# Where a three-mixer trunk runs its weight-stream k-tiles, and which engine applies the rotary sine

## What is computed

```python
for l in range(DEPTH):                       # DEPTH = 2
    mod = (silu(c) @ w_ada[l] + b_ada[l])    # six vectors of 1024 per sequence
    h = rmsnorm(x, norm_mix[l]) * (1 + sc_m) + sh_m
    proj = h @ w_in[l]
    o_a = gated_delta(silu(conv4(q_a, k_a, v_a)), g, beta)     # A
    q_b = _rope(q_b, pos); k_b = _rope(k_b, pos) * HEAD_K ** -0.5
    o_b = retention(q_b, k_b, v_b)                             # B
    o_c = hgrn2(q_c, f_gate, v_c)                              # C
    o_i = norm(o_i) * gate_i                                   # each, per head
    merged = sum(sigmoid(merge_i) * (o_i @ w_branch[l, i]))
    x = x + gt_m * (merged @ w_out[l])
    h = rmsnorm(x, norm_ffn[l]) * (1 + sc_f) + sh_f
    x = x + gt_f * ((silu(h @ wg) * (h @ wu)) @ w_down[l])
# _rope: concatenate([x1 * cos - x2 * sin, x1 * sin + x2 * cos])
```

## Time and profile before

| | us |
|---|---|
| three executions | 2683.02, 2673.51, 2682.92 |
| their median | 2682.92 |
| the profiled execution | 2676.24 |
| its span, first to last instruction | 2674.2 |
| PE busy | 2516.4 (94%) |
| POOL busy | 1546.2 (58%) |
| DVE busy | 1015.0 (38%) |
| ACT busy | 456.3 (17%) |
| mean granted TensorE clock | 0.967 of full |

### The profile page before, as it was taken

The page is one execution under the profiler, slowest core; times in us unless marked ns, Lnnn a source line. Parts: engine busy times, 40 slices in busy tenths (PEclk is TensorE's granted clock), DMA queues, the critical chain, the costliest instruction groups (busy, mean ns, idle before and its releaser), DMA issues. The chain is left out here.

```text
span 2674.2 us, 47818 instructions
## 1 busy us (share of the span) xinstructions
PE 2516.4 (94%) x20318; PEld 2404.7 (90%) x20318; DVE 1015.0 (38%) x1479; ACT 456.3 (17%) x856; POOL 1546.2 (58%) x1292
## 2 busy tenths in 40 slices
PE   6989999999999899999989899999999998999997
PEld 4879888989989899999978799799899798999997
DVE  3663424150743442222255633421427435222223
ACT  3421222121121120000034222310211212000001
POOL 2542235557547757777755322355664486777775
PEclk8999999999999999999989899999999898999999
DMA  8720014223324512322365210142241142223222
GB/s 350 243 80 28 29 41 126 65 64 106 93 58 132 208 64 91 85 90 89 87 225 184 64 34 28 47 123 76 64 138 50 55 152 64 89 87 90 87 87 77
DMA packets 167043, 263.92 MB, mean 99 GB/s; under 512 B 14128, under 2 KB 83376, under 8 KB 165040
## 3 DMA queue, kind: packets, MB, share of 16 engines
q1 hardware_dynamic: 166832, 260.88, 30.9%
HBM read 239.65 MB, written 21.17 MB: 98 GB/s over the span
## 5 line engine op out<-in xcount | busy, mean ns | idle before, releaser
L796 PE MATMUL gemm_psum<-h_hi_lo,w_hi_lo 128*128 128x272 f32 x12000 | 1626.3, 294 | 42.5 <-DVE h_hi_lo L1326 31.6
L796 PEld LDWEIGHTS gemm_psum<-h_hi_lo,w_hi_lo 128*128 128x128 f32 x12000 | 1557.9, 193 | 89.6 <-issue 78.7
L525 POOL TENSOR_TENSOR w_hi_lo<-w_raw,consts 128x512 fp32r<-128x512 f32 (+1 forms) x644 | 691.7, 1074 | 1052.2 <-PE gemm_psum L796 966.9
L527 POOL TENSOR_TENSOR w_hi_lo<-w_raw,w_hi_lo 128x512 fp32r<-128x512 f32 (+1 forms) x644 | 855.8, 1329 | 50.4
L1970 ACT ACTIVATE tiles<-gemm_psum 128x544 f32<-128x544 f32 (+1 forms) x188 | 116.3, 623 | 1184.7 <-PE gemm_psum L796 1184.1
L796 PE MATMUL gemm_psum<-ffn_hi_lo,w_hi_lo 128*128 128x272 f32 x2112 | 264.8, 287 | 0.0
L796 PEld LDWEIGHTS gemm_psum<-ffn_hi_lo,w_hi_lo 128*128 128x128 f32 x2112 | 264.4, 188 | 0.0
L1952 DVE TENSOR_TENSOR tiles<-gemm_psum,tiles 128x544 f32<-128x544 f32 x44 | 31.9, 725 | 386.7 <-PE gemm_psum L796 376.2
L796 PE MATMUL gemm_psum<-o_hi_lo,w_hi_lo 128*128 128x272 f32 x1152 | 154.0, 290 | 0.0
L796 PEld LDWEIGHTS gemm_psum<-o_hi_lo,w_hi_lo 128*128 128x128 f32 x1152 | 147.1, 189 | 0.0
L1970 ACT ACTIVATE scratch<-mix_psum 128x512 f32<-128x512 f32 (+3 forms) x112 | 58.9, 547 | 359.7 <-PE mix_psum L1073 174.8
(11 more groups left out here) (234 smaller groups left out, 1915.0 us busy)
## 6 DMA issues: line engine op xcount, KB each, us to landing
w_raw<-in_w_gu SPq DMA_DIRECT2D x176, 256.0 KB, 2.7
tiles<-in_w_ada SPq DMA_DIRECT2D x64, 512.0 KB, 4.9
w_raw<-in_w_merge SPq DMA_DIRECT2D x96, 256.0 KB, 2.6
w_raw<-in_w_first SPq DMA_DIRECT2D x68, 256.0 KB, 5.2
w_raw<-in_w_ret SPq DMA_DIRECT2D x64, 256.0 KB, 2.7
w_raw<-in_w_hg SPq DMA_DIRECT2D x64, 256.0 KB, 2.7
w_raw<-in_w_dn SPq DMA_DIRECT2D x64, 256.0 KB, 2.6
w_raw<-in_w_merge SPq DMA_DIRECT2D x96, 128.0 KB, 2.1
```

Source lines behind the costliest of these rows:

```text
L525: pool.tensor_tensor(hi, src, ones[:, 0:1].broadcast_to([P, words]), ALU.mult).then_inc(hi_done, 1)
L527: pool.tensor_tensor(lo, src, hi.bitcast(F32), ALU.subtract).then_inc(split_done, 1)
L796: mm = pe.matmul(GP[:, 2 * (tile % 2) + h, 0:HALF], whl[:, n % SLOTS, a, j * P:(j + 1) * P], rhs[:, b, step, h * HALF:(h + 1) * HALF], sta ...
```

## The change

Five things, the same in both layers except where said.

1. The fills of mixer A are bounded by `RG_END`, no more by `Z_END`, and more k-tiles stand in them: 4 for 2 ahead of the last join, 5 for 2 ahead of `branch_ready`, 4 for 2 ahead of the query products of each pair of chunks. The `drain(Z_END)` ahead of the sampled chunk is gone. The fills ahead of the sum of squares in the three norms are 2, 4, 6 for 2, and those behind it 7, 6, 5 for 3.
2. The sine product of a `rope` tile moves from DVE to POOL, behind the split of the fourth slab after that tile. DVE adds the two products one tile later, tile 7 with the first `gdn_z` tile.
3. The copy of the gate columns (L1520 before) moves ahead of the last convolution.
4. DVE waits for the stored prompt state inside `start_branch`, behind `branch_ready`.
5. POOL splits slabs 1 to 3 of layer 0 in the layer's block, not in the first block. SP loads the four ada groups with 16 k-tiles of stream between them, and the first one eight k-tiles earlier in its list.

```diff
+SUMS_FILL = (2, 4, 6)
+ROOT_FILL = (7, 6, 5)
...
         def _(pool):
             pool.wait_ge(sig("ones_landed"), 16)
-            for n in range(SLOTS):
-                split_slab(pool, n)
+            split_slab(pool, 0)
...
-                fill(4 * H + KD, BASE["silu0"])
+                fill(4 * H, BASE["silu0"])
                 if ahead:
                     sp.wait_ge(sig("h_ready"), 2 * KD)
                     for i in range(4):
                         sp.dma_start(ada_group[i], w_ada_first[l + 1, i]).then_inc(sig(f"ada_group_landed_{i}"), 16)
+                        fill(2 * KD, BASE["silu0"])
...
             def _(pool):
+                for n in range(1, SLOTS if l == 0 else 0):
+                    split_slab(pool, n)
                 for n in range(slab_base + SLOTS, slab_end):
                     split_slab(pool, n)
+                    for i in range(8):
+                        if n == slab_base + last_slab(BASE["rope"] + i) + SLOTS:
+                            tmp = swap_temp[i % 2]
+                            pool.wait_ge(sig("swapped"), i + 1)
+                            pool.tensor_tensor(tmp, tmp, C[:, C_SIN:C_DRET], ALU.mult).then_inc(sig("sine_applied"), 1)
...
-                    fill(2, limit)
+                    fill(SUMS_FILL[n], limit)
                     four_sums(sq_o[n], 0, True, True)
-                    fill(3, limit)
+                    fill(ROOT_FILL[n], limit)
...
                     i = TILES[tile][1]
                     wait_tile(tile)
                     k.next(sig("swapped"))
-                    out, tmp = brt[:, RQ + i, :], swap_temp[i % 2]
-                    dve.tensor_tensor(halves(out), gp(tile), halves(C[:, C_COS:C_SIN]), ALU.mult
-                                      ).then_inc(buf_free[tile % 2], 1)
-                    k.link(dve.tensor_tensor(tmp, tmp, C[:, C_SIN:C_DRET], ALU.mult))
+                    k.link(dve.tensor_tensor(halves(brt[:, RQ + i, :]), gp(tile), halves(C[:, C_COS:C_SIN]), ALU.mult))
+                    release_buffer(tile)
+                    if i:
+                        rope_sum(i - 1)
+
+                def rope_sum(i):
+                    out = brt[:, RQ + i, :]
+                    k.next(sig("sine_applied"))
                     k.settle()
-                    dve.tensor_tensor(out, out, tmp, ALU.add).then_inc(sig("rope_slot_free"), 1)
+                    dve.tensor_tensor(out, out, swap_temp[i % 2], ALU.add).then_inc(sig("rope_slot_free"), 1)
...
                     say("branch_ready")
+                    if stored:
+                        dve.wait_ge(sig("stored_prompt"), 16 * stored)
                     k.link(dve.memset(ST[:, :, :], 0.0))
...
                 def gdn():
-                    fill(2, Z_END)
+                    fill(5, RG_END)
```

More of the change, by code:

```diff
@@ L1010, in _ @@
                         per_head(3, lambda c: pe.transpose(B[:, 3, c * P:(c + 1) * P], ROW[:, cols(c)], ident))
-                fill(2, Z_END)
+                fill(4, RG_END)
                 ada_join(ADA_LOTS - 1)
@@ L1021, in _ @@
                         four_spreads(j, half)
-                        fill(2, Z_END)
+                        fill(2, RG_END)
                 def gdn_turn(c):
@@ L1365, in _, with release_buffer @@
                 sum_base = [0]
+                def release_buffer(tile):
+                    k.settle()
+                    dve.nop().then_inc(buf_free[tile % 2], 1)
                 def rope(tile):
@@ L1406, in evacuate @@
                         rope(tile)
+                    elif tile == BASE["gdn_z"]:
+                        rope_sum(7)
                     elif name == "hg_f":
@@ L1483, in gate_rows, with columns_of @@
                     say("gate_rows_ready")
+                def columns_of(bank, parts):
+                    return bank.rearrange("p (c j x) -> p c j x", j=4, x=32)[0:parts, :, 0:3, 0:4]
                 for n in range(1, NCQ + 1):
@@ L1507, in _ @@
                         rows_of()
+                        k.next(full[3])
+                        k.link(dve.tensor_copy(COL[:, 0:NCH, :].rearrange("p c (j x) -> p c j x", j=3), columns_of(B[:, 3, :], P)))
+                        release(3)
                 def bank_pair(i):
@@ L1513, in bank_pair @@
                     return B[:, b:b + 2, 0:HALF], b
-                def columns_of(bank, parts):
-                    return bank.rearrange("p (c j x) -> p c j x", j=4, x=32)[0:parts, :, 0:3, 0:4]
-                fill(2, Z_END)
-                k.next(full[3])
-                k.link(dve.tensor_copy(COL[:, 0:NCH, :].rearrange("p c (j x) -> p c j x", j=3), columns_of(B[:, 3, :], P)))
-                release(3)
+                fill(4, RG_END)
                 k.next(full[2])
@@ L1548, in _, with start_branch @@
                         release_four()
-                        fill(2, Z_END)
+                        fill(2, RG_END)
                 k.next(sig("gate_exps"))
                 k.link(dve.tensor_tensor(CE[:, :, 8:12], CE[:, :, 0:4], COL[:, :, 4:8], ALU.mult))
-                def start_branch(tiles):
+                def start_branch(tiles, stored=0):
                     k.settle()
@@ L2027, in evacuate @@
                     elif name == "ret_v":
+                        act.wait_ge(sig("rope_slot_free"), 10)
                         take(tile, brt[:, RV + i, :], ACT.Copy)
```

57 lines of the change are left out of this document (26 added, 31 removed).

## The result

The changed kernel takes 2651.69 us, the median of four executions (2650.57 to 2652.75), where the kernel before takes 2681.53 (2673.51 to 2683.02, four executions, one more than shown above). The medians are 30 us apart. The ratio given for them is 0.9906, with a 95% interval of 0.9878 to 0.9935, which is 25 us, as much as the span fell in the profiled executions. So the gain is 25 to 30 us, where the forecast had 46, and the forecast of 2636 was 15.7 too low. The range holds the time. The number is nearest to the rival in which the clock stays low (2656), but not by that rival's way: it wanted all 26.6 us of the waits and nothing of the clock. That the two add up to nearly its number is luck.

A forecast was written before the change was run, and what follows sets the result against it. PE was taken as the bound, with its waits and lower clock as the time to gain. Waits 24.8 + 6.4 - 4.6 + clock 19.6 = 46.2 us off the median of 2682.9 gave 2636.7, stated as 2636; range 2604 to 2664.

The forecast's parts named there:

- the rival in which the clock stays low: Whole run: the waits left bring the lower clock back, so only 26.6 us are gained, giving 2656; chance 0.15.
- entry of A: Ahead of mixer A's gate columns, per layer: two k-tiles fit into the 3.71 us wait; waits fall by 1.8.
- rope tiles 0 and 1: Fourth spread and `branch_ready` in mixer A, per layer: these tiles end earlier, ahead of awaited steps; waits rise by 2.1 us.
- products: First pair in mixer A, per layer: tile 1 no longer delays the query products, tile 2 delays the next step; 0.7 us gained.
- levels and second pair: Mixer A, per layer: fewer delays from rope tiles; 0.6 us gained in the levels and 1.2 in the second pair.
- norm of A: Norm of mixer A, per layer: four more k-tiles cover the 2.47 us wait for the rows; 2.5 gained.
- start of B: Start of mixer B, per layer: DVE's 2.42 us wait for the stored state moves behind `branch_ready` and is covered; 2.4 gained.
- norm of B: Norm of mixer B, per layer: k-tiles take in 3.8 us, but `hg_f` tiles delay the root and state products; 1.0 gained.
- norm of C: Norm of mixer C, per layer: four more k-tiles cover the 2.88 us wait, two the 1.54; 4.3 gained.
- `w_out`: Among the `out` tiles, once: with the ada groups spaced out, the 6.38 us wait goes; 6.4 gained.
- start (first k-tile): Start of layer 0, once: it starts 2.3 us earlier, but POOL's six operations among DVE's cost 6.9; net 4.6 lost.
- clock, both layers: Fourteen half-clock stretches of 1.4 us go, six per layer in the mixers, two behind the 6.38 wait; 19.6 gained.

The follow-up runs named there:

- e2: The changed kernel with 3 k-tiles ahead of the sums in the norm of B, not 4, and 7 behind them, not 6: 2639.5 us.
- e8: The changed kernel with 4, 3, 6 k-tiles ahead of the norms' sums, 7 behind each, and POOL splitting slabs 0 to 2 in the first block: 2626.3 us.
- e4: The changed kernel with 3 k-tiles ahead of the turns of mixer A, not 5, on PE, DVE and ACT: 2653.9 us.
- e7: The changed kernel with the norms' fills of the kernel before, 2 k-tiles ahead of the sums and 3 behind in each: 2657.4 us.
- e3: The changed kernel with the sine product back on DVE, both products and the addition of a rope tile in one place: 2663.6 us.
- e11: The changed kernel without the sine on POOL, the new norm fills, the moved slab splits and the spaced ada groups: 2679.4 us, ratio 1.0006 to the kernel before.

## Why the prediction was right, and where it was wrong

The direction, the range and most places of the new waits were right. The sum was 21 too high (46.2, where the span fell by 25.0). Of its own signs two failed: the 1.64 left at the spreads of C, where it wanted under 0.5, and the clock of 0.970, where it wanted 0.975. By its own steps, waits of layer 0 in us, gains positive, from the brackets of before and after:

| step | predicted | measured |
|---|---|---|
| entry of A | 1.8 | 0.9 (3.71 to 2.85) |
| rope tiles 0 and 1 | -2.1 | -2.4 (3.26 to 1.55 + 4.07) |
| products | 0.7 | 0.4 (4.49 to 2.35 + 1.74) |
| levels and second pair | 1.8 | 2.3 |
| norm of A | 2.5 | 0.9 (2.47 to 1.54) |
| start of B | 2.4 | 2.4 (2.42 to 0) |
| norm of B | 1.0 | -4.1 (3.65 to 5.25 + 2.49) |
| norm of C | 4.3 | 2.8 (4.42 to 1.64) |
| `w_out` | 6.4 | 6.4 |
| start (first k-tile) | -4.6 | -2.3 |
| clock, both layers | 19.6 | 7.9 (15.8 of half-clock time in the traces) |

The measured waits of two layers, with the 6.4 and the -2.3, make 10.5 of the 12.0 by which PE's idle time fell.

**Norm of B, the largest miss among the waits.** The step said that `hg_f` tile 0 would end just ahead of the sums and that DVE's three operations would precede the reciprocal. Both happened. Two things failed. The step's sum doesn't follow from its own figures: a reciprocal 2.0 later leaves 3.65 + 2.0 - 3.8 = 1.9 of wait at the norm's own steps, and with 3.5 at the state products that is 5.4 where 3.65 stood, so 1.7 lost and not 1.0 gained. And the size: the reciprocal was to start 2.0 later and started 4.1 later (561.72 after 557.63), though the stage began 1.2 sooner (484.89 after 486.05), because the gate products ahead of it took 6.21 beside two of POOL's splits and not 4.25 beside one, and the three operations 3.6. The wait for the rows grew from 2.33 to 5.25. At the state products 3.5 were foreseen, and 2.49 came. e2 shows that this placement alone costs 11 us in the two stages of its trace, and some 12 by the times.

**Norms of A and C.** At A the 2.47 went, as predicted, and 1.54 came ahead of it, at the sums. There the last `ret_v` tile now stands ahead of the squares in ACT's queue, and ACT waits until PE has finished it:

```profile
408.15 0.62 ACT L1987 ACTIVATE tiles<-gemm_psum 128x544 f32<-128x544 f32 x1 [6.16 <-PE gemm_psum L805]
```

ACT starts the squares at 408.67, 1.8 behind DVE's last operation for them. In the kernel before it was 0.2. The step had looked only for tiles that DVE empties. At C the step counted k-tiles and not DVE's queue. The gate products took 5.28 beside splits (3.33 before), and the reciprocal, at 790.07, stood behind them:

```profile
784.57 5.28 DVE L1657 TENSOR_TENSOR tiles<-tiles 128x544 f32<-128x544 f32 x4 [0.29 <-DVE scratch L1415]
```

That put it off by 1.0, as ACT's root had ended at 788.94. The rest lies in the row that the step took. The 1.54 was short because PE's three k-tiles ahead of it took 3.22 at the lower clock; the same wait in layer 1 of the kernel before was 2.33. In e8, with two more k-tiles at each of the two places, both brackets are gone.

**The start.** The mechanism was right, the term of 6.9 for six operations put in between was too large: DVE's part took 4.6 longer, 0.25 to 1.07 for each of the six operations that met a split. By the Trainium skill (SBUF — State Buffer, section SBUF: two separate sides) an operation of VectorE with two SBUF inputs is held by a GpSimd operation that reads SBUF, so all seven should be held where a split runs, and an operation on one input outside the 2-port modes should not. The trace agrees with both, as far as the reciprocal is of the second kind, which no run shows by itself: 0.42 became 1.37, the seventh operation, behind the last split, took 0.75 as before, and the reciprocal at 160.78 took 3.54 while POOL's splits ran beside it, as long as elsewhere (3.55).

**The clock, the largest miss of all.** Fourteen stretches of 1.4 us were to go. Four went: the trace of the kernel before has 31 stretches at the lower clock, that of the changed kernel 27. The step took each as bound to its wait, so that fewer waits mean fewer stretches. Executions of one kernel speak against that: on one chip the kernel before had 155 to 188 us of half-clock time in eleven executions, at 2667.6 to 2680.9 us. So do equal waits, as in the two layers of e4. The norm of B has brackets of 1.32 and 2.33 in the kernel before, of 1.33, 2.33 and 0.59 in e7. Here is the stretch from 551 to 586 us, columns as above, of the kernel before:

```profile
551.00:586.00 35.00, 31.35 (x196) 25.39 (x195) 24.54 (x25) 13.63 (x24) 15.18 (x12) 0.85 0.12 38
```

And of e7:

```profile
551.00:586.00 35.00, 30.74 (x226) 25.40 (x225) 28.27 (x28) 13.64 (x24) 17.70 (x14) 1.00 0.14 46
```

At 0.85 PE got 196 matmuls done, at 1.00 226. So what a wait costs is itself plus a draw that the wait alone doesn't settle. What settles it no run here shows. Of the 13.0 that PE's busy time fell, the clock explains 7.9. The other 5.1 I can't assign.

**What the prediction had not priced.** The sine product on POOL appeared as one operation less where PE waits. It is worth 13 us (16 by the ratios), nearly all through the clock (e3), while the order of A, for which the sum had 9.2 and more, gains nothing without it (e11). So the terms of mixer A belonged to the two edits together, not to the fills alone.

## What to carry to other kernels

Place filler work by what ends in it, not by its amount: at each wait, list the tiles whose last piece falls ahead of it, on every engine that empties one (ACT's too), and put the piece that completes a tile behind the awaited operation. Move only the engine whose queue is in the way, and look what it then stands in front of. Count the clock as part of the price of small waits, but only by whole executions, several of each kernel: a term that adds up half-clock stretches wait by wait is not good to better than 10 us here.
